# A hybrid decoder layer on one core: the linear attention's first two levels copied by another engine, its chunk states taken in one piece, and the sample products moved behind later work

## The chip, the core and the metric

The kernel runs on one core of a Trainium2 chip. The core has a matrix engine (PE, TensorE), a vector engine (DVE), an activation engine (ACT), a general engine (POOL) and a queue engine (SP) that starts DMAs. PE writes only to PSUM, which this program uses as four units of 128 partitions by 1024 floats, `unit[0]` to `unit[3]`. Each engine works through its own list of instructions in order, and the lists meet only at semaphores. The metric is the device time of one launch in microseconds; lower is better.

## What is computed

One inference step of a decoder layer for 512 prompt tokens and for 8 running sequences with 4 new tokens each ("samples"), 544 rows of width 1024. Cut to what matters here:

```python
h = x @ w_in                                        # one projection, 2320 columns
gk = log_sigmoid(g_lr @ w_gk_up + b_gk_up) / 16
# gated linear attention, 4 heads, key width 64, value width 128
S_t = diag(exp(gk_t)) S_{t-1} + k_t^T v_t ;  o_t = q_t S_t
o_gla = rms_norm(o_gla) * silu(o_gate)
o_swa = sink_attention(...)                         # window of 128 keys
x1 = layer_norm(ALPHA * x + concat(o_gla, o_swa) @ w_out)
x2 = layer_norm(ALPHA * x1 + moe(x1))               # top 4 of 32 experts
```

All products are in fp32. The recurrence also returns its last state, for the prompt and for each sample sequence.

## The kernel before

Five stages follow each other on PE: the input projections with the window attention woven in (up to 207 us of the profiled execution), the linear attention (to about 260 us), the output projection with the first layer norm and the router (to about 355 us), and then 32 experts, each with three products of 1024 by 1024 weights that stream through a ring of 16 buffers. The change touches only what lies between about 195 us and 290 us.

**Levels.** The attention matrix of a 128-token chunk is built without large exponents: for each of seven block sizes (`LEVELS`, 64 down to 1), DVE forms the exponents' arguments (`level_args(j)`), ACT takes the exponential (`level_exp(j)`), DVE multiplies keys and queries by it into `kE` and `qR` (`level_ops(j)`, which raises `ops_ready`), PE multiplies them (`level(j)`, 16 small matmuls, L1029), and DVE copies the blocks of that size under a mask into `attT` (`level_in(j)`, L2156). `E`, `kE` and `qR` exist twice, for even and odd levels. The diagonal of `attT` is written by ACT beforehand (`diagonals`, 16 copies of the identity scaled by `qkdot`), as is the samples' small `attS`. When the last level is in, DVE raises `att_ready`.

**Chunk states.** `chunk_state(i)` (L1049) multiplies the decayed keys `er` by the values `gv` for chunk i; DVE's `state_in(i)` adds them up with decay into `state`. In the kernel before they alternate with the levels, on PE and on DVE.

**Outputs.** `within_chunk(i)` (L1112) is `attT` times `gv`, `from_state(i)` (L1122) is `qe` times `state`; the samples get `sample_carried` (L1062, L1067: `qbm` times the carried state `s0`) and four products with `attS` (L1131). ACT squares each output for the norm, DVE's `norm_gate(i)` scales it. In the order 0, 1, 2, 4, 3 (`MIXED`; 4 is the samples) the rows are transposed (`mix_T`, L752), copied by ACT (`mix_in`) and multiplied by `wo` (`out_product`, L1157, L1161). `sample_state` (L1080, `kdm` times `gv`) gives the samples' new states, which DVE's `sample_state_in` adds and POOL writes out; `kdm` comes from ACT's `by_sequence`. SP starts the experts' weights only when all outputs so far are written (`out_done`).

**Units.** Which PSUM unit a result takes is written out in the tables `LATE` and `TAIL`: a result waits until the one before it in its unit has been read. At the projections' end units are released by ACT's copies of the last columns (`proj_copy(4)`, into `gv`).

ACT, PE and DVE weave pieces of the attention between the projections' steps: `piece(p)` runs after half steps, p from 0 to 39. The lines below set ACT's order at the projections' end:

```python
                if p == 37:
                    qk_in(1)
                    qk_in(2)
                    diagonals()
                if p == 38:
                    qk_in(3)
                    qk_in(4)
                    level_exp(0)
                    ...
                    by_sequence(0)
                    by_sequence(1)
```

Of the kernel before, what the change touches and what calls it, by code (L numbers as in the profile page):

```python
# [54 lines left out]
LATE = ["level0", "level1", "ds0", "level2", "ds1", "level3", "ds2", "level4", "ds3", "level5", "level_s0", "level6",  # L55
        "level_s1", "go0", "go1", "go2", "go3"]
TAIL = ["mixT0", "mixT1", "sds0", "sds1", "out0", "mixT2", "out1", "mixT4", "x1T0", "mixT3", "out2", "logit0", "x1T1", "out4", "logit1",
        "out3", "x1T2", "logit2", "x1T4", "x1T3", "logit4", "logit3"]
ORDER = ([(f"x{i}", i % 4) for i in range(NT)] + [(name, n % 3) for n, name in enumerate(LATE)] + [("go4", 3)]
         + [(name, (2, 0, 3, 1)[n % 4]) for n, name in enumerate(TAIL)]  # L60
# [59 lines left out]
def build(nc, d):  # L120
    with ExitStack() as ctx:
# [360 lines left out]
        def _(sp):  # L482
# [38 lines left out]
            sp.dma_start(res[:, 0:2], d["x_prompt"][0, 0:2 * P].rearrange("(i p) d -> p i d", p=P)).then_inc(res_in, 16)  # L521
# [220 lines left out]
        def _(pe):  # L742
# [299 lines left out]
            def chunk_state(i):  # L1042

                name = f"ds{i}"
                pe.wait_ge(*emptied(name))
                pe.wait_ge(products, NT + 2)
                for h in range(GH):
                    a, q = divmod(h, 2)
                    ins = mm(bank(name)[64 * q:64 * q + 64, a * GDV:(a + 1) * GDV], er[:, i, h * 64:(h + 1) * 64],  # L1049
                             gv[:, i, h * GDV:(h + 1) * GDV], start=True, stop=True)  # L1050
                ins.then_inc(s_full(name), 1)
# [19 lines left out]
            def sample_state(half):  # L1071

                name = f"sds{half}"
                pe.wait_ge(*emptied(name))
                pe.wait_ge(operands, 1 + half)
# [16 lines left out]
            chunk_state(1)  # L1092
            level(3)
            chunk_state(2)
            level(4)
            chunk_state(3)
            level(5)
            level(6)
            banks_free((6, 7))
            sample_carried()  # L1100
# [27 lines left out]
            within_chunk(2)  # L1128
            for h in range(GH):
# [4 lines left out]
            from_state(1)  # L1134
            from_state(2)
# [43 lines left out]
            mix_T(1)  # L1179
            sample_state(0)  # L1180
            sample_state(1)
            out_product(0)
# [226 lines left out]
        def _(act):  # L1409
# [195 lines left out]
            def diagonals():  # L1605
                act.wait_ge(used1, NIN - 2)
                act.wait_ge(qkdot_ready, 1)
                for n in range(16):
# [13 lines left out]
            def piece(p):  # L1622
# [28 lines left out]
                if p == 36:  # L1651
                    qk_in(0)
                if p == 37:
                    qk_in(1)
                    qk_in(2)
                    diagonals()
                if p == 38:
                    qk_in(3)
                    qk_in(4)
                    level_exp(0)  # L1660
                    act.wait_ge(*has(f"o{NS2 - 1}"))
                    act.wait_ge(products, NT + 2)
                    by_sequence(0)
                    by_sequence(1)
# [217 lines left out]
        def _(v):  # L1882
# [196 lines left out]
            def piece(p):  # L2079
# [27 lines left out]
                if p == 38:  # L2107
# [3 lines left out]
                    level_ops(0)  # L2111

# [60 lines left out]
            def state_in(i):  # L2173
                name = f"ds{i}"
                v.wait_ge(*filled(name))
                src = bank(name)[:, 0:2 * GDV].rearrange("p (a e) -> p a e", a=2)
# [8 lines left out]
                v.sem_inc(s_freed(name), 1)  # L2185
# [14 lines left out]
            for j in range(7):  # L2200
                if j + 2 < 7:
                    level_args(j + 2)
                if j + 1 < 7:
                    level_ops(j + 1)
                if j == 0:
                    v.wait_ge(operands, 3)
                level_in(j)
                if j == 0:
                    st(tt(qe[:], qkT[:, 0:2], eb[:], ALU.mult), queries_ready)
                    v.wait_ge(queries_ready, 2)  # L2210
                    st(tt(qbm[:], qe[:, :, SEQ:T].unsqueeze(2).to_broadcast([P, 2, NSEQ, NS]),
                          c_("colseq").rearrange("p (n t) -> p n t", n=NSEQ).unsqueeze(1)
                          .to_broadcast([P, 2, NSEQ, NS]), ALU.mult), queries_ready)
                if 1 <= j <= PT:
                    state_in(j - 1)
# [23 lines left out]
            sample_state_in(0)  # L2239
            sample_state_in(1)  # L2240
            v.wait_ge(res_in, 48)
# [58 lines left out]
            first_norm(0)  # L2300
            first_norm(1)
            first_norm(2)
# [303 lines left out]
```

## Time and profile before

| | us |
|---|---|
| median of 3 runs | 1477.77 |
| lowest, highest | 1475.67, 1478.14 |
| profiled execution, its own time | 1478.91 |
| its span, first to last instruction | 1476.8 |
| PE busy | 1401.0 (95%) |
| DVE busy, ACT busy | 470.9, 322.1 |

The profiled execution took 2.1 us more than its span; that part lies outside the instructions. Its own time is 1.1 us above the median of the runs. Times within the span are counted from the first instruction. PE is busy nearly everywhere, but the share is an average: in the stretch that the change touches it is lower, and PE runs there at half clock for most of the time.

### The profile page before, as it was taken

To read this page: it belongs to the slowest core of one execution; us is meant where nothing else is said; L and a number is where in the kernel's file an instruction comes from. 1 tells how busy PE (TensorE), PEld (TensorE's weight loads), DVE (VectorE), ACT (ScalarE), POOL (GpSimd) and SP (SyncE) were. 2 spreads that over 40 slices of the span, in tenths; PEclk is the share of its full clock that TensorE was granted. 3 is DMA by queue.
4 is the path that set the end of the run, shared out by engine and by line. 5 is a ranking of instruction groups with operands and counts; after the bars stand their busy time and mean duration, and the time that the engine had idled before them with its cause. 6 is when DMAs were issued, how large, how long until landed. Compare 5 with 4: busy or idle time off the path is not lost.

```text
span 1476.8 us, 37700 instructions
## 1 busy us (share of the span) xinstructions
PE 1401.0 (95%) x16570; PEld 956.8 (65%) x16570; DVE 470.9 (32%) x895; ACT 322.1 (22%) x662; POOL 116.0 (8%) x119
## 2 busy tenths in 40 slices
PE   6999979997999999999999999999999999999991
PEld 5777768555566666666666666666666666666660
DVE  3245547356232222223222222222322222222223
ACT  2544453321111112111111111111111111211114
POOL 1022000000010000000000000100000000010000
PEclk9999986995999999999999999999999999999996
DMA  7311032626899999999999999999999999999934
GB/s 230 101 48 44 15 122 87 246 104 252 333 373 397 400 398 396 400 390 394 399 394 395 396 399 402 398 395 391 402 399 388 397 399 398 399 401 395 389 159 143
DMA packets 78469, 463.93 MB, mean 314 GB/s; under 512 B 12401, under 2 KB 13633, under 8 KB 29009
## 3 DMA queue, kind: packets, MB, share of 16 engines
q1 hardware_dynamic: 67616, 429.54, 73.0%
q0 software_dynamic: 10192, 31.31, 8.3%
q8 instruction: 132, 2.16, 0.6%
q10 hardware_dynamic: 512, 0.79, 0.1%
q14 instruction: 17, 0.13, 0.0%
HBM read 444.70 MB, written 22.22 MB: 316 GB/s over the span
## 4 chain that ended last, share of the span: by engine, by line
PE 89%; ACT 4%; DVE 4%; DMA 2%; issue 2%; DVEq 0%; POOL 0%; ACTq 0%; SPq 0%; POOLq 0%
PE unit L1248 41%; PE unit L1251 27%; PE unit L1157 4%; PE unit L1231 2%; PE unit L757 2%; PE unit L1236 2%; PE unit L759 2%; PE unit L758 2%; PE unit L752 1%; PE unit L1175 1%; DMA xbuf<-x_prompt_dram 1%; PE unit L909 1%; PE unit L885 1%; PE unit L792 1%; PE unit L1029 0%
## 5 line engine op out<-in xcount | busy, mean ns | idle before, releaser
L1248 PE MATMUL unit<-ring_b,xeT 128*32 128x512 f32 (+1 forms) x3168 | 353.3, 488 | 1.1 <-ACT xeT L1411 1.1
L1251 PE MATMUL unit<-ring_b,xeT 128*32 128x256 f32 x1584 | 353.8, 381 | 0.0
L1251 PE MATMUL unit<-ring_a,xeT 128*32 128x256 f32 x1488 | 330.7, 379 | 0.0
L1248 PE MATMUL unit<-ring_a,xeT 128*32 128x256 f32 (+1 forms) x2976 | 330.2, 486 | 0.0
L1251 PEld LDWEIGHTS unit<-ring_b,xeT 128*32 128x32 f32 x1584 | 171.3, 110 | 56.3 <-issue 0.7
L1251 PEld LDWEIGHTS unit<-ring_a,xeT 128*32 128x32 f32 x1488 | 161.8, 110 | 52.5
L1251 PE MATMUL unit<-ring_a,heT 128*32 128x256 f32 x768 | 169.7, 379 | 0.0
L1248 PE MATMUL unit<-ring_a,heT 128*32 128x512 f32 (+1 forms) x1536 | 169.4, 486 | 0.0
L1248 PEld LDWEIGHTS unit<-ring_b,xeT 128*32 128x32 f32 x3168 | 126.4, 110 | 60.4 <-issue 4.0
L1251 PE MATMUL unit<-ring_b,heT 128*32 128x256 f32 x720 | 160.3, 379 | 0.0
L1248 PE MATMUL unit<-ring_b,heT 128*32 128x256 f32 (+1 forms) x1440 | 160.1, 486 | 0.0
L1248 PEld LDWEIGHTS unit<-ring_a,xeT 128*32 128x32 f32 x2976 | 120.1, 110 | 51.7 <-issue 2.5
L1411 ACT ACTIVATE heT<-unit 128x768 f32<-128x768 f32 x31 | 25.2, 812 | 509.6 <-PE unit L1236 509.6
L2427 DVE TENSOR_TENSOR hb<-unit,brow 128x768 f32<-128x768 f32 x32 | 30.6, 958 | 305.1 <-PE unit L1251 305.1
L2397 DVE TENSOR_TENSOR gm<-unit,brow 128x768 f32<-128x768 f32 x32 | 30.7, 958 | 233.1 <-PE unit L1251 233.1
L1251 PEld LDWEIGHTS unit<-ring_a,heT 128*32 128x32 f32 x768 | 84.3, 110 | 27.1
L694 POOL DMA_INDIRECT acc_rows<-ysb,idx x32 | 46.6, 1455 | 682.4 <-ACT ysb L1802 682.4
L1251 PEld LDWEIGHTS unit<-ring_b,heT 128*32 128x32 f32 x720 | 79.2, 110 | 25.4
L1798 ACT ACTIVATE ysb<-unit,gcol 96x768 f32<-96x768 f32 x32 | 28.7, 898 | 250.2 <-PE unit L1251 250.2
L1248 PEld LDWEIGHTS unit<-ring_a,heT 128*32 128x32 f32 x1536 | 63.0, 110 | 28.8 <-issue 0.9
L1248 PEld LDWEIGHTS unit<-ring_b,heT 128*32 128x32 f32 x1440 | 59.2, 110 | 27.9
L2327 DVE TENSOR_TENSOR row_part<-unit,ck 96x3 f32<-96x3 f32 x32 | 5.0, 155 | 209.3 <-PE unit L1225 209.3
(319 smaller groups left out, 1619.7 us busy)
## 6 DMA issues: line engine op xcount, KB each, us to landing
ring_b<-w_gate_dram SPq DMA_DIRECT2D x68, 1024.0 KB, 17.7
ring_a<-w_down_dram SPq DMA_DIRECT2D x68, 1024.0 KB, 18.2
ring_b<-w_up_dram SPq DMA_DIRECT2D x64, 1024.0 KB, 17.1
ring_a<-w_up_dram SPq DMA_DIRECT2D x64, 1024.0 KB, 18.4
ring_a<-w_gate_dram SPq DMA_DIRECT2D x60, 1024.0 KB, 17.6
ring_b<-w_down_dram SPq DMA_DIRECT2D x60, 1024.0 KB, 17.4
raw_a<-w_in_dram SPq DMA_DIRECT2D x16, 512.0 KB, 3.6
xbuf<-x_prompt_dram SPq DMA_DIRECT2D x4, 512.0 KB, 5.6
```

Source lines behind the costliest of these rows:

```text
L694: return pool.indirect_dma_start(acc_dram, bass.IndirectOffsetOnAxis(ap=at, axis=0), out, None, compute_op=ALU.add)
L757: mm(out, xh, wh, start=start, stop=False)
L758: mm(out, xh, wl, start=False, stop=False)
L759: return mm(out, xl, wh, start=False, stop=stop)
L1157: ins = mm(bank(name)[:, h * HALF:(h + 1) * HALF], mix[i % 2][:, k], wo[:, k, h * HALF:(h + 1) * HALF], start=k == 0, stop=k == KD - 1)
L1231: ins = tr(px[:, k * P:k * P + CAP], half, ident[:CAP, :CAP])
L1236: ins = tr(px[:, k * P:(k + 1) * P], gm[:, k * P:(k + 1) * P], ident)
L1248: return mm(out[j * NS:(j + 1) * NS, a:b], stat(j), w[:, a:b], start=first, stop=last)
L1251: return mm(out[CAP:P, j * 256:(j + 1) * 256], stat(j), w[:, FOLD:D], start=start, stop=stop)
L1798: nc.scalar.activation(ysb[:CAP, 0:FOLD], pd[:CAP, 0:FOLD], ACT.Identity, scale=gcol[:CAP, par:par + 1])
L2397: tt(gm[:], pg[:, 0:FOLD], brow[:, 0], ALU.add).then_inc(h_part, 1)
L2427: tt(hb[:], pu[:, 0:FOLD], brow[:, 1], ALU.add).then_inc(h_part, 1)
```

## The change

ACT's order at the projections' end is new: the diagonals are written in two halves, one after `qk_in(0)` and one ahead of `qk_in(1)`; `level_exp(0)` goes ahead of `qk_in(3)`; `by_sequence` moves behind all the exponentials. ACT copies levels 0 and 1 into `attT` itself with plain copies (`coarse_in`), two of 64x512 for level 0 and four of 32x256 for level 1; DVE does levels 2 to 6 as before. DVE computes `qe` right after the first `level_ops`, and `qbm` and the sums of the chunk states behind the levels. On PE the four chunk states form one piece between level 0 and level 1, in unit 3, which holds nothing else then. `sample_carried` moves from ahead of the outputs to behind `from_state(2)`, and `sample_state` from ahead of `out_product(0)` to behind it; DVE's `sample_state_in` moves behind the first norm. The first load of `res` signals another semaphore, so that the first two norms wait for it alone. The core of the diff:

```diff
-LATE = ["level0", "level1", "ds0", "level2", "ds1", "level3", "ds2", "level4", "ds3", "level5", "level_s0", "level6",
-        "level_s1", "go0", "go1", "go2", "go3"]
+LATE = [f"level{j}" for j in range(6)] + ["level_s0", "level6", "level_s1", "go0", "go1", "go2", "go3"]
...
             banks_free((0, 1))
             level(0)
+            banks_free((4, 5, 6, 7))
+            pe.wait_ge(proj_out, 5)
+            chunk_states()
             banks_free((2, 3))
-            level(1)
-            banks_free((4, 5))
-            pe.wait_ge(proj_out, 5)
-            chunk_state(0)
-            level(2)
...
+            for j in range(1, 7):
+                level(j)
             pe.wait_ge(att_ready, 1)
...
                 if p == 36:
                     qk_in(0)
+                    diagonals(0)
                 if p == 37:
+                    diagonals(1)
                     qk_in(1)
                     qk_in(2)
-                    diagonals()
                 if p == 38:
+                    level_exp(0)
                     qk_in(3)
                     qk_in(4)
-                    level_exp(0)
-                    act.wait_ge(*has(f"o{NS2 - 1}"))
-                    act.wait_ge(products, NT + 2)
-                    by_sequence(0)
-                    by_sequence(1)
...
+            def coarse_in(j):
+
+                half, name = LEVELS[j], f"level{j}"
+                act.wait_ge(*filled(name))
+                for q in range(2):
+                    src = bank(name)[:, q * HALF:(q + 1) * HALF].rearrange("p (b n r) -> p b n r", b=8, r=half)
+                    for n in range(64 // half):
+                        own = slice(2 * half * n, 2 * half * n + half)
+                        st(copy(attT[own, 8 * q:8 * q + 8, own.stop:own.stop + half], src[own, :, n]))
+                st.settle()
+                act.sem_inc(s_freed(name), 1)
+
+            level_exp(1)
+            level_exp(2)
+            coarse_in(0)
+            level_exp(3)
+            coarse_in(1)
             for n in range(4):
                 ins = copy(attS[:, n], ident[:NS, :NS], scale=qkdot[:NS, 16 + n:17 + n])
                 st(ins, operands if n == 3 else None)
-            for j in range(1, 7):
+            for j in range(4, 7):
                 level_exp(j)
+            act.wait_ge(*has(f"o{NS2 - 1}"))
+            act.wait_ge(products, NT + 2)
+            by_sequence(0)
+            by_sequence(1)
...
                 if j + 1 < 7:
+                    if j:
+                        v.wait_ge(*filled(f"level{j - 1}"))
                     level_ops(j + 1)
...
+                if j > 1:
+                    level_in(j)
+            for i in range(PT):
+                state_in(i)
...
             first_norm(0)
+            sample_state_in(0)
+            sample_state_in(1)
             first_norm(1)
+            v.wait_ge(res_in, 32)
             first_norm(2)
```

The first place is PE, from its first level to its first output product. In the kernel before its instructions stand so (`qR`, `kE` are a level, `gv,er` a chunk state, `s_118` the carried sample state, `gv,attT` the outputs within a chunk, `state,qe` those from the state, `gv,kdm` the new sample states):

```order
L1029 MATMUL unit<-qR,kE 128x64 x16
L1029 MATMUL unit<-qR_122,kE_121 128x64 x16
L1049 MATMUL unit<-gv,er 64x128 x4
L1029 MATMUL unit<-qR,kE 128x64 x16
L1049 MATMUL unit<-gv,er 64x128 x4
...
L1062 MATMUL unit<-s_118,zeros 32x256 x2
L1067 MATMUL unit<-s_118,qbm 32x128 x32
L1112 MATMUL unit<-gv,attT 128x128 x12
L1131 MATMUL unit<-gv,attS 32x128 x4
L1122 MATMUL unit<-state,qe 128x128 x8
```

In the changed kernel the same stretch of PE's list begins with all chunk states behind the first level, and the samples' products follow the outputs of chunks 0 to 2:

```order
L1028 MATMUL unit<-qR,kE 128x64 x16
L1049 MATMUL unit<-gv,er 64x128 x16
L1028 MATMUL unit<-qR_122,kE_121 128x64 x16
L1028 MATMUL unit<-qR,kE 128x64 x16
...
L1103 MATMUL unit<-gv,attT 128x128 x12
L1113 MATMUL unit<-state,qe 128x128 x8
L1062 MATMUL unit<-s_118,zeros 32x256 x2
L1067 MATMUL unit<-s_118,qbm 32x128 x32
L1125 MATMUL unit<-gv,attS 32x128 x4
L1103 MATMUL unit<-gv,attT 128x128 x4
```

The matmuls are the same in kind and number; the 16 of the chunk states now stand together ahead of level 1, and 34 sample matmuls stand behind `att_ready` instead of ahead of it.

The second place is ACT at the projections' end. In the kernel before, the diagonals, the keys by sequence (`kdm`) and the copies of the last projection (`gv`) stand so:

```order
L1411 ACTIVATE qTa<-unit 128x4x128 x3
L1411 ACTIVATE attT<-ck,qkdot 128x128 x16
L1411 ACTIVATE qTa<-unit 128x4x128
L1411 ACTIVATE qTa<-unit 128x4x32
L1620 ACTIVATE E<-E 128x2x512
L1411 ACTIVATE kdm<-er,ce 32x256 x8
L1411 ACTIVATE gv<-unit 128x512 x4
L1411 ACTIVATE gv<-unit 32x128 x4
L1411 ACTIVATE attS<-ck,qkdot 32x32 x4
L1620 ACTIVATE E_120<-E_120 128x2x512
```

In the changed kernel:

```order
L1403 ACTIVATE qTa<-unit 128x4x128
L1403 ACTIVATE attT<-ck,qkdot 128x128 x16
L1403 ACTIVATE qTa<-unit 128x4x128 x2
L1612 ACTIVATE E<-E 128x2x512
L1403 ACTIVATE qTa<-unit 128x4x128
L1403 ACTIVATE qTa<-unit 128x4x32
L1403 ACTIVATE gv<-unit 128x512 x4
L1403 ACTIVATE gv<-unit 32x128 x4
L1612 ACTIVATE E_120<-E_120 128x2x512
L1612 ACTIVATE E<-E 128x2x512
L1403 ACTIVATE attT<-unit 64x8x64 x2
```

The 16 diagonal copies stand two copies earlier, the first exponential two copies earlier, and nothing stands any more between the copies of the queries and keys (`qTa`) and those of the last projection.

## Rows read from the trace of the kernel before

**Rows 1.** Windows of PE: start:end, length, PE busy (count), clock share, DMA, GB/s

```profile
207.30:250.90 43.60, 33.23 (x302) 0.53 0.50 173
...
283.30:337.00 53.70, 53.59 (x240) 1.00 0.43 167
...
403.00:1476.00 1073.00, 1041.97 (x14017) 0.99 0.98 379
```

**Rows 2.** Chain that ended last, 186 to 272 us: start, length, what

```profile
201.17 4.80 ACT attT L1411 x16
...
207.93 3.28 ACT kdm L1411 x8
211.21 2.07 ACT gv L1411 x5
```

**Rows 3.** Timeline of ACT: start, length, line, operation, idle before and releaser

```profile
194.82 0.60 ACT L1411 ACTIVATE qTa<-unit 128x512 f32<-128x512 f32 x1 [0.69 <-PE unit L918]
199.67 1.32 ACT L1411 ACTIVATE qTa<-unit 128x512 f32<-128x512 f32 x2 [4.25 <-PE unit L918]
...
206.96 1.06 ACT L1620 ACTIVATE E<-E 128x1024 f32<-128x1024 f32 x1
```

**Rows 4.** Timeline of PE: last projection steps, a level, a state, outputs, products

```profile
202.67 0.96 PE L918 MATMUL unit<-ck,qk 128*128 128x128 f32 x8
...
206.55 0.65 PE L792 MATMUL unit<-raw_a,xs 128*32 128x128 f32 x16
212.26 3.68 PE L1029 MATMUL unit<-qR,kE 64*128 64x64 f32 x32 [5.07 <-ACT gv L1411]
...
221.93 1.12 PE L1049 MATMUL unit<-gv,er 128*64 128x128 f32 x8
...
248.88 4.31 PE L1067 MATMUL unit<-s,qbm 64*32 64x128 f32 x64
253.12 2.94 PE L1112 MATMUL unit<-gv,attT 128*128 128x128 f32 x24
255.99 1.06 PE L1131 MATMUL unit<-gv,attS 32*32 32x128 f32 x8
...
259.62 0.71 PE L1122 MATMUL unit<-state,qe 64*128 64x128 f32 x8
...
263.96 3.98 PE L1080 MATMUL unit<-gv,kdm 32*64 32x128 f32 x64 [0.47 <-DVEq L2231]
267.87 15.38 PE L1157 MATMUL unit<-wo,mix_a 128*128 128x512 f32 x32
...
283.96 13.90 PE L1157 MATMUL unit<-wo,mix_b 128*128 128x512 f32 x32
```

**Rows 5.** Timeline of DVE: qe, arguments, masked copies, one chunk state, the last level

```profile
219.82 1.29 DVE L2209 TENSOR_TENSOR qe<-qTa,eb 128x1088 f32<-128x1088 f32 x1
...
227.37 0.69 DVE L2059 TENSOR_TENSOR E<-cum 128x512 f32<-128x512 f32 x1
...
229.64 1.31 DVE L2156 COPY_PREDICATED attT<-ce,unit 128x512 f32<-128x512 int32 x2
231.11 0.61 DVE L2181 SCALAR_TENSOR_TENSOR state<-state,eb,unit 128x128 f32<-128x128 f32 x2 [0.16 <-DVE attT L2156]
...
247.93 2.43 DVE L2156 COPY_PREDICATED attT<-ce,unit 128x512 f32<-128x512 int32 x2 [1.02 <-PE unit L1029]
250.50 0.31 DVE L2167 COPY_PREDICATED attS<-ce,unit 32x32 f32<-32x32 int32 x2
```

**Rows 6.** Windows of PE around its clock changes, columns as in group 1

```profile
207.00:212.00 5.00, 0.19 (x8) 0.72 0.69 229
...
248.00:251.00 3.00, 3.00 (x40) 0.63 0.98 381
```

**Rows 7.** Timelines of POOL and SP: the sample states' store, the first weights

```profile
271.56 1.17 POOL L654 DMA_DIRECT2D st_s_dram<-s x1 [28.20 <-DVEq L2194]
...
277.69 1.99 SPq L543 DMA_DIRECT2D ring_b<-w_gate_dram x4
```

More of the change, by code:

```diff
@@ L520, in _ @@
             sp.wait_ge(*has("kq4"))
[L521 removed]
+            sp.dma_start(res[:, 0:2], d["x_prompt"][0, 0:2 * P].rearrange("(i p) d -> p i d", p=P)).then_inc(x_in[0], 16)
             sp.wait_ge(ops_ready, 7)
@@ L1040, in level, with chunk_states @@
                     ins.then_inc(s_full(name), 1)
-            def chunk_state(i):
-                name = f"ds{i}"
-                pe.wait_ge(*emptied(name))
+            def chunk_states():
+                pe.wait_ge(*emptied("ds"))
                 pe.wait_ge(products, NT + 2)
[L1047 to L1051, printed above, removed]
+                for i in range(PT):
+                    for h in range(GH):
+                        a, q = divmod(h, 2)
+                        at = i * 2 * GDV + a * GDV
+                        ins = mm(bank("ds")[64 * q:64 * q + 64, at:at + GDV], er[:, i, h * 64:(h + 1) * 64],
+                                 gv[:, i, h * GDV:(h + 1) * GDV], start=True, stop=True)
+                ins.then_inc(s_full("ds"), 1)
             def sample_out(a, q):
@@ L1074, in sample_state @@
                 pe.wait_ge(*emptied(name))
-                pe.wait_ge(operands, 1 + half)
+                pe.wait_ge(operands, 2 + half)
                 for n in range(4 * half, 4 * half + 4):
@@ L1128, in _ @@
             within_chunk(2)
+            from_state(1)
+            from_state(2)
+            sample_carried()
             for h in range(GH):
@@ L1179, in _ @@
             mix_T(1)
+            out_product(0)
             sample_state(0)
             sample_state(1)
-            out_product(0)
             mix_T(2)
@@ L1603, in qk_in, with diagonals @@
                 act.sem_inc(s_room(name), 1)
-            def diagonals():
-                act.wait_ge(used1, NIN - 2)
+            def diagonals(half):
+                act.wait_ge(used1, NIN - 3 + half)
                 act.wait_ge(qkdot_ready, 1)
-                for n in range(16):
+                for n in range(8 * half, 8 * half + 8):
                     st(copy(attT[:, n], ident, scale=qkdot[:, n:n + 1]))
@@ L2173, in state_in @@
             def state_in(i):
-                name = f"ds{i}"
-                v.wait_ge(*filled(name))
-                src = bank(name)[:, 0:2 * GDV].rearrange("p (a e) -> p a e", a=2)
+                v.wait_ge(*filled("ds"))
+                src = bank("ds")[:, i * 2 * GDV:(i + 1) * 2 * GDV].rearrange("p (a e) -> p a e", a=2)
                 if i == 0:
@@ L2203, in _ @@
                 if j + 1 < 7:
+                    if j:
+                        v.wait_ge(*filled(f"level{j - 1}"))
                     level_ops(j + 1)
[L2205 to L2215, printed above, removed]
+                if j == 5:
+                    v.wait_ge(operands, 1)
+                if j == 2:
+                    v.wait_ge(*emptied("level3"))
+                    v.wait_ge(*emptied("level4"))
+                if j > 1:
+                    level_in(j)
+            for i in range(PT):
+                state_in(i)
+            v.wait_ge(queries_ready, 2)
+            st(tt(qbm[:], qe[:, :, SEQ:T].unsqueeze(2).to_broadcast([P, 2, NSEQ, NS]),
+                  c_("colseq").rearrange("p (n t) -> p n t", n=NSEQ).unsqueeze(1)
+                  .to_broadcast([P, 2, NSEQ, NS]), ALU.mult), queries_ready)
             def norm_gate(i):
```

25 lines of the change are left out of this document (7 added, 18 removed).

## The prediction, made before the changed kernel ran

> **What bounds the kernel now.** I read the kernel by stretches first. From 403 us to the end PE is busy 1041.97 of 1073 us at full clock, and none of that code changes [rows 1]. From 283.3 to 337 us PE is busy 53.59 of 53.70 us: a time won before 283 us is handed on unchanged through the output products. Between 207.3 and 250.9 us it is different: PE is busy 33.2 of 43.6 us at a clock share of 0.53, so the levels are bound by something else [rows 1]. The chain of what ended last says by what. Up to about 216 us it runs through ACT: the 16 diagonals from 201.17 us for 4.80 us, `kdm` for 3.28 us, the `gv` copies from 211.21 us [rows 2]. PE had ended the projections at 207.2 us and waited 5.07 us, until 212.26 us, for a `gv` copy that frees its unit [rows 4]. From 216 us to 240 us the chain runs through DVE, which does four things for each level: arguments, operands, masked copy, chunk state. From 253 us PE's outputs take over.
>
> So there are three places to price: the start of level 0, the length of the levels up to `att_ready` (250.9 us, when the last `attS` copy of 250.50 us has ended [rows 5]), and PE's path from there to the first output product at 267.87 us [rows 4]. I make the sum against the profiled execution, 1478.91 us with a span of 1476.8, which stands 1.1 us above the median of the runs, 1477.77.
>
> **Start of level 0.** On ACT the copy of 194.82 us ends at 195.4 [rows 3]. The diagonals follow it at once, since their inputs have been there for long, and take 4.8 us as before [rows 2], to 200.3. Two `qTa` copies take 1.32 [rows 3], to 201.6, and the exponential 1.06 [rows 3], to 202.7. PE's transposes for the last two copies run from 202.67 to 203.6 [rows 4]; these copies end at about 204.3, and the `gv` copies of at most 0.6 us (five took 2.07 us, the last ones small [rows 2]) can follow the projections as they come. Level 0 needs units 0 (banks 0 and 1), free at about 205.7, and its operands: DVE starts at 204.3 and takes 1.3 for the wide `kE` (as `qe`, 1.29 for as many columns [rows 5]) and 0.7 for `qR`: 206.4. PE itself is the last, at 207.2 [rows 4]. Level 0 starts at 207.4 us, not 212.26: **4.9 us** earlier.
>
> **Levels.** DVE continues: `qe` 1.3 (207.7), arguments of level 1 behind the projections' end (209.2), arguments of level 2 (210.7), operands 1 (212.7), arguments 3 (214.2), operands 2 (215.6), arguments 4 (217.1). A pair of 0.69 us instructions with its wait is 1.4 to 1.5 us [rows 5]. PE: level 0 takes 3.68 us at half clock [rows 4]; the clock was still full until about 209 us in the row that has 0.72 for 207 to 212 us [rows 6], so I take half of it, 1.9 us, to 209.3. The 16 products of the chunk states follow: four took 1.12 us at half clock [rows 4], so 4.5 us, to 213.8. PE holds level 1 back by that: 213.8 to 217.5, level 2 to 221.2. Operands 3 overwrite the operands of level 1 and wait for it: 219.0. DVE's first masked copy, level 2, runs 221.2 to 222.7. ACT's six coarse copies are 2 times 0.6 and 4 times about 0.4 (between the 0.6 us for 512 columns and 0.27 for the small `gv` copies [rows 2]), 2.8 us in all, on an engine that is idle there; level 1's end at about 219.2, ahead of 221.2.
>
> From there DVE does 4.45 us a level (three parts) where it did 5.3 (four; a state is 0.61 plus its waits, 0.85 [rows 5]): level 3 in at 227.1, level 4 at 231.6, operands 6 at 233.1. Level 5 is filled at 233.8; its two masked copies last 2.43 us, the small ones 0.31 [rows 5]: in at 236.9. PE fills level 6 at 237.9, and it is in at **241.0**, against 250.9: 9.9 us earlier, the first 4.9 included. Bounds: had level 0 run at half clock as well, everything from level 1 on would be 1.8 us later (242.8); had PE kept full clock through the states and level 1, DVE alone would set the pace and `att_ready` come at 238.4. I take the middle because the clock had fallen at about 209 us only after PE had stood idle from 207.2, and PE is not idle there now.
>
> Here a rule can be held against the trace. PE was busy in 33.2 of 43.6 us, three quarters of the stretch, yet its clock share was 0.53 in it; it rose only at the stretch's very end, in the row of 248 to 251 us, which has 0.63 [rows 1, 6]. The Trainium skill, TensorE: Matmul & The Clock Gate (Part 1), says that the clock gate opens by how busy PE has been recently. By that sentence the denser levels would soon run at full clock, and `att_ready` would come at the 238.4 us of the bound above, 2.6 us earlier than in my sum; the two rows speak against it.
>
> **From `att_ready` to the first product.** Before, it takes from 250.9 to 260.3 us, when the last `from_state` (259.62 plus 0.71) ends: 9.4 us [rows 4]. The samples' carried products had run under DVE's last copies. Now they stand behind `att_ready`, and all is serial on PE: outputs of three chunks 2.9, two `from_state` 1.3 (0.6 to 0.7 each), the carried products 4.1 (5.0 before with the zero products, of which 2.2 us lay at half clock), `attS` 1.0, the last chunk's outputs 1.0, its `from_state` 0.6 [rows 4]: 10.9 us at full clock. DVE's four states (3.2 us) and `qbm` (0.7 us) are done at 245.0, before PE wants them. `go0`'s norm frees its unit at about 248, well ahead of the last chunk. But PE comes to this work at half clock, where before the clock had risen at 250 us under the samples' products. Bounds for the loss: 0 to all of it at half clock (below, a rival). I take 5 us at half clock, so 2.5 us, because the row of 248 to 251 us shows the rise within some 2 us of such products. End: 241.0 + 10.9 + 2.5 = 254.4, against 260.3: **5.9 us** left of the 9.9.
>
> Then the transposes. Before, three waits for DVE's norms made it 3.6 us from 260.3 to 263.96 [rows 4]. Now the norms of chunks 0 to 2 are long done; the two transposes take 2.2 us, and ACT, behind the squares of chunk 3 (to 255.7), has copied the first at 256.8. `out_product(0)` starts 2.4 us after 254.4: **1.2 us** more.
>
> **Products.** The 3.98 us of new sample states and the product swap places at the same cost. The first product took 15.3 us (to 283.2) where the later took 13.8, for PE started it at half clock [rows 4]. It now follows denser work, but the sample states may bring the same fall ahead of the second product. Between 0 and 1.5 us of gain I take 0.8.
>
> **What is hidden.** The sample states' sum moves behind the first norm, which ends at about 277 us, so their store is issued at about 280 us and not 271.56, and SP starts the experts' weights at about 286, not 277.69 [rows 7]. Seven buffers of 1 MB follow; PE wants the first at about 361, so this costs nothing. The second load of `res` waits for the sample states, too, about 6 us later than before, at 275; the store of the same megabyte was written 6.1 us after its issue [rows 7], and the third norm wants the load at about 305. Only if the cover of over 60 us were gone would this be paid in full. SP's queue holds nothing else there, and POOL's next task waits for the transpose of the samples' rows anyway.
>
> Sum: 9.9 from start and levels, less 4.0 by which the path behind `att_ready` grows (13.4 against 9.4), and 1.2 and 0.8: 7.9, rounded to **8.0 us**. 1478.9 - 8.0 = 1470.9 in a profile, 1477.8 - 8.0 = **1469.8 us** as a median.
>
> **Rivals.** (a) *Smaller gain.* All levels at half clock, level 0 too (-1.8), half clock for 8 us behind `att_ready` (-1.5), the same fall in a product (-0.8): a gain of 3.9 us, 1473.9. For it speaks the share of 0.53 in the whole stretch [rows 1]. Chance 0.24. (b) *Larger gain.* PE stays at full clock until level 1 and rises at once behind `att_ready`: 2.6 + 1.5 more, 12 us, 1465.8. Against it speaks the same row. Chance 0.13. (c) *Slower.* The clock stays low right through the outputs. Then 10.9 us become 21.8 from 242.8, to 264.6; transposes and copy 3.5, product 15.3, states 5: 288.4 against the 283.2 of before, 5 us slower, 1483. It decides from about 16 us more of half clock than my 5. For it speaks that levels that keep PE busy for three quarters of 43.6 us did not raise the clock [rows 1]; against it that it rose within some 2 us of sample products [rows 6]. Chance 0.07. (d) *No change*, within 0.2% (3 us, about what a measurement of this kernel can tell): the win is made but is taken back by something with a fixed time behind it. I find only the weights' DMA, with 60 us of cover. Chance 0.06. My forecast, a gain of 6 to 10 us, has 0.50.
>
> **How the numbers follow.** Faster by over 0.2% are the forecast, (a) but for a rest, and (b): 0.86 with the cut; same 0.07; slower 0.07. The range goes from the larger gain (1466.0) to somewhat under the smaller one (1474.8), and leaves out (c), (d) and the extremes.
>
> **What would show it.** Level 0 at about 207.4 us; DVE without masked copies until 221; PE's level 1 held by the chunk states until about 214; `att_ready` between 238.4 and 242.8; the first output product at about 257 us. A first level 0 later than 209 us, a coarse copy that ends after level 2 is filled, or a clock share near 0.5 between 245 and 257 us would make the prediction wrong.

## The result

The changed kernel took 1463.41 us in the median of 5 runs (1462.03 to 1467.1), the kernel before 1477.77 us (5 runs, 1474.71 to 1479.71). The ratio, which goes by the means, is 0.9913, with a 95% interval of 0.990 to 0.9926: 12.9 us faster, between 11 and 15. The medians are 14.4 us apart. I had forecast 1469.8 us, a gain of 8.0, and a range from 1466.0 to 1474.8. The direction was right, the gain was over half as large again as forecast, and the median lies below the range. The profiled execution took 1466.54 us.

The page of the changed kernel, its first two parts in extract (busy time, then tenths in 40 slices):

```profile
span 1464.6 us, 37705 instructions
## 1 busy us (share of the span) xinstructions
PE 1394.1 (95%) x16570; PEld 952.6 (65%) x16570; DVE 467.8 (32%) x891; ACT 325.1 (22%) x668; POOL 116.0 (8%) x119
...
PEclk8999996995999999999999999999999999999996
```

The span is 12.2 us shorter, and PE's busy time fell by 7 us although it does the same matmuls: some of them now run at full clock. DVE lost 3 us of copies and ACT gained 3, as the diff says.

The timeline of PE, from the end of the projections to the first output product (start, length, line, operation, and in brackets the idle time before it with its releaser); it answers to [rows 4]:

```profile
205.16 0.64 PE L791 MATMUL unit<-raw_a,xs 128*32 128x128 f32 x16
206.20 2.00 PE L1028 MATMUL unit<-qR,kE 64*128 64x64 f32 x32 [0.40 <-issue]
208.13 1.97 PE L1049 MATMUL unit<-gv,er 128*64 128x128 f32 x32
211.18 2.00 PE L1028 MATMUL unit<-qR,kE 64*128 64x64 f32 x32 [1.08 <-DVEq L2087]
214.14 6.63 PE L1028 MATMUL unit<-qR,kE 64*128 64x64 f32 x64 [0.95 <-DVEq L2087]
...
237.26 5.21 PE L1103 MATMUL unit<-gv,attT 128*128 128x128 f32 x24 [2.80 <-DVEq L2182]
242.40 1.16 PE L1113 MATMUL unit<-state,qe 64*128 64x128 f32 x16
...
249.61 0.71 PE L1113 MATMUL unit<-state,qe 64*128 64x128 f32 x8
...
252.81 13.97 PE L1149 MATMUL unit<-wo,mix_a 128*128 128x512 f32 x32 [0.59 <-ACT mix_a L1403]
266.71 3.71 PE L1080 MATMUL unit<-gv,kdm 32*64 32x128 f32 x64
```

Level 0 follows the projections after 0.4 us; before, it was 5.06. Level 0, the 16 chunk-state products and level 1 took 2.00, 1.97 and 2.00 us: all three at full clock. The windows of PE say when that ended (length, PE busy, clock share, DMA):

```profile
212.00:214.00 2.00, 1.18 (x22) 1.00 1.04 391
214.00:216.00 2.00, 1.86 (x23) 0.68 1.02 340
216.00:218.00 2.00, 2.00 (x22) 0.50 1.08 297
...
240.00:242.00 2.00, 2.00 (x11) 0.50 0.20 63
242.00:244.00 2.00, 2.00 (x26) 0.99 0.04 10
```

The clock fell at about 214.7 us, 8.9 us behind the projections' end, where before it had fallen 2.0 us behind it. It rose again at 242, 4.8 us into the outputs. The timeline of DVE, which answers to [rows 5], shows what came of the full clock:

```profile
215.59 0.69 DVE L2082 TENSOR_TENSOR kE<-qTa,E 128x512 f32<-128x512 f32 x1 [0.22 <-DVE E L2069]
216.20 0.68 DVE L2085 TENSOR_TENSOR qR<-qTa,E 128x512 f32<-128x512 f32 x1
217.45 1.31 DVE L2167 COPY_PREDICATED attT<-ce,unit 128x512 f32<-128x512 int32 x2 [0.56 <-PE unit L1028]
```

The first masked copy begins 11.25 us behind level 0's start; in my sum it was 13.8. The two groups of ACT's own copies, in its timeline:

```profile
210.18 1.07 ACT L1403 ACTIVATE attT<-unit 64x512 f32<-64x512 f32 x2
...
213.47 1.55 ACT L1403 ACTIVATE attT<-unit 32x256 f32<-32x256 f32 x4
```

They took 2.6 us together, against 2.8 in the sum, and were over at 215.0 us, ahead of level 2.

I compare kernels below by stages of one profile each, read from such timelines: the projections' end (end of the last product with the samples' rows), level 0's start, `att_ready` (end of the last `attS` copy), the end of the last `from_state`, the starts of the first and second output products, the experts' first product, the end of the span. All in us.

| kernel | projections end at | to level 0 | to att_ready | to last from_state | to 1st product | to 2nd product | to experts | projections' end to the end |
|---|---|---|---|---|---|---|---|---|
| before | 207.20 | 5.06 | 38.55 | 9.52 | 7.54 | 16.09 | 86.08 | 1269.60 |
| changed | 205.80 | 0.40 | 30.86 | 13.26 | 2.49 | 18.47 | 85.96 | 1258.80 |
| my sum | 207.2 | 0.2 | 33.6 | 13.4 | 2.4 | 19.4 | as before | 1261.6 |

(The last row's last entry is 1269.60 less the forecast 8.0.) Behind the projections the gain is 10.8 us; the other 1.4 us of the profiles' difference lie ahead of them, where the change moves only ACT's diagonals and first exponential.

### The profile page after: what moved, and what is told of

Same layout as the page of the kernel before. It is cut to its first block, busy times and chain, and to the rows that moved or that the text cites. A ratio compares the mean times of both kernels' runs of the same rounds, so it can differ in the third digit from the quotient of the medians.

```text
span 1464.6 us, 37705 instructions
## 1 busy us (share of the span) xinstructions
PE 1394.1 (95%) x16570; PEld 952.6 (65%) x16570; DVE 467.8 (32%) x891; ACT 325.1 (22%) x668; POOL 116.0 (8%) x119
## 4 chain that ended last, share of the span: by engine, by line
PE 90%; DVE 3%; ACT 3%; DMA 2%; issue 1%; DVEq 0%; POOL 0%; SPq 0%; ACTq 0%; POOLq 0%
PE unit L1240 42%; PE unit L1243 27%; PE unit L1149 4%; PE unit L1223 2%; PE unit L756 2%; PE unit L1228 2%; PE unit L758 2%; PE unit L757 2%; PE unit L751 1%; PE unit L1167 1%; PE unit L1028 1%; DMA xbuf<-x_prompt_dram 1%; PE unit L908 1%; PE unit L884 1%; PE unit L791 1%
```

## The experiments

Each kernel is the changed one with one edit, unless said otherwise. The stages, in the columns of the table above:

| kernel | projections end at | to level 0 | to att_ready | to last from_state | to 1st product | to 2nd product | to experts | projections' end to the end |
|---|---|---|---|---|---|---|---|---|
| before, again | 206.61 | 5.07 | 38.56 | 9.54 | 7.52 | 16.11 | 85.87 | 1269.59 |
| changed, again | 203.17 | 0.42 | 30.94 | 13.17 | 2.49 | 18.47 | 85.94 | 1258.53 |
| ACT's order undone | 203.84 | 5.08 | 30.87 | 12.75 | 2.48 | 18.47 | 85.95 | 1262.86 |
| coarse copies on DVE | 206.65 | 0.42 | 33.40 | 13.60 | 2.49 | 19.78 | 86.76 | 1264.55 |
| DVE's sums between levels | 206.48 | 0.39 | 32.64 | 12.44 | 2.49 | 18.47 | 85.90 | 1259.22 |
| states twice | 206.24 | 0.39 | 30.56 | 13.37 | 2.49 | 20.09 | 87.41 | 1261.86 |
| levels 0 to 2 and states twice | 206.23 | 0.40 | 34.49 | 13.17 | 2.49 | 18.47 | 85.97 | 1262.37 |
| matmuls into PE's waits | 201.96 | 0.40 | 33.38 | 11.01 | 2.48 | 18.71 | 87.32 | 1260.74 |
| new states first | 202.02 | 0.40 | 31.37 | 12.36 | 5.47 | 14.71 | 85.86 | 1257.58 |
| new states first, again | 206.36 | 0.40 | 30.82 | 13.30 | 5.48 | 16.36 | 85.85 | 1259.24 |
| early samples | 203.70 | 0.39 | 30.89 | 10.58 | 3.87 | 19.07 | 86.85 | 1259.10 |
| early samples, new states first | 205.98 | 0.43 | 30.96 | 10.47 | 7.10 | 14.71 | 85.19 | 1255.72 |

**The changed kernel again.** No edit.

> The changed kernel, unedited, for a second profile and more times. Two theories on why its first profile gained 12.2 us where 8.0 were forecast. Clock theory: about 2.4 us come from PE's clock staying full until level 2 (level 0 to att_ready took 31.0 us) and 1.7 us from a first output product and sample states without a half clock; both are there again, within 1.5 us. Chance theory: about 1.4 us lie ahead of 193 us, in the first loads of x, and vary from run to run, and the five first times (1462.0 to 1467.1) differ by that or by where the clock falls; then from level 0 to the experts' first product this profile stays within 1 us of the first (151.0 us), and the rest of the difference lies in the start and in the time of the clock's last rise.

Median 1466.02 us of 4 runs (1463.67 to 1467.98), ratio to before 0.9926 (0.9905 to 0.9948). From level 0 to the experts 151.01 us, against 151.04 in the first profile, the clock's fall and rise included. What differs is ahead of it: 2.6 us. So the spread of the runs lies in the start, as the chance theory had it, and the gain behind the projections is there again. Why it is there a repetition cannot say.

**The kernel before again.** No edit.

> The kernel before, unedited, for a second profile. In its first the projections ended at 207.2 us; in five profiles of changed kernels, whose code up to there is the same but for ACT's diagonals, they ended at 202.0 to 206.7 us. Chance theory: this one, too, ends them anywhere from 202 to 208 us, and from there to the end it takes 1269.6 us again, within 1 us. Rival: the change itself makes the start shorter, and it ends them at 207 us again.

1478.16 us. Behind the projections 1269.59 us, against 1269.60. The projections ended at 206.6 us, within the spread of 202.0 to 206.7 us of the changed kernels, though in its upper part, which fits both theories. Where the start's time goes shows in the windows from 150 to 180 us. Of the kernel before:

```profile
150.00:180.00 30.00, 27.61 (x159) 0.89 0.05 17
```

Of the changed kernel's second profile:

```profile
150.00:180.00 30.00, 27.55 (x165) 0.94 0.00 1
```

And of the kernel with new states first, where the code up to there is the same:

```profile
150.00:180.00 30.00, 27.56 (x173) 1.00 0.00 1
```

The projection step that runs between 159 and 176 us took 16.8, 15.4 and 13.8 us in these three. PE has waits of 0.65 and 1.45 us there while ACT and DVE take in the output gate and go on with the window attention, and the clock falls for some 7 us, some 3 us or not at all. These steps of about 1.5 us, with up to 2.6 us gathered before that step, make up the spread. Of the 2.6 us, 1.6 lie ahead of the first product of the projections, which waits for the first loads. Both profiles of before had the longest step, the two of the changed kernel one longest and one middle. With the two stages apart, the change is worth 10.8 to 11.1 us; the rest of the 12.9 lies ahead of them, where profiles of one and the same kernel spread by over 4 us. Whether ACT's earlier diagonals shift those chances stays open: 9 of 14 profiles had the longest step, and only two are of before's code.

**ACT's order undone.** This separates the late level 0 from the clock, since PE then stands idle ahead of it as before.

```diff
                 if p == 36:
                     qk_in(0)
-                    diagonals(0)
                 if p == 37:
-                    diagonals(1)
                     qk_in(1)
                     qk_in(2)
+                    diagonals(0)
+                    diagonals(1)
                 if p == 38:
-                    level_exp(0)
                     qk_in(3)
                     qk_in(4)
+                    level_exp(0)
+                    act.wait_ge(*has(f"o{NS2 - 1}"))
+                    act.wait_ge(products, NT + 2)
+                    by_sequence(0)
+                    by_sequence(1)
...
```

> ACT's order at the projections' end as before, all else as changed: diagonals behind the copies of p 37, the first exponential behind those of p 38, keys by sequence ahead of the gv copies. By my prediction level 0 starts 4.9 us later against the end of the projections (5 us behind it). Clock theory adds: PE stands idle for 5 us, so its clock falls ahead of level 0, and level 0 to att_ready takes about 3 to 4 us more than the 31.0 us of the changed kernel, since level 0 (3.7), the states (4.5) and level 1 run at half clock. In all about 8 us later at att_ready. Rival: the levels are paced by DVE alone, and it takes 31 us again, 5 us later in all.

1468.63 us. Level 0 started 5.08 us behind the projections, 4.7 later, as both theories had it. But `att_ready` came after the same 30.87 us: the clock theory's extra 3 to 4 us did not come. The timeline of PE in this kernel:

```profile
208.92 3.68 PE L1028 MATMUL unit<-qR,kE 64*128 64x64 f32 x32 [5.08 <-ACT gv L1403]
212.53 3.68 PE L1049 MATMUL unit<-gv,er 128*64 128x128 f32 x32
216.14 5.91 PE L1028 MATMUL unit<-qR,kE 64*128 64x64 f32 x96
```

And DVE's first masked copy:

```profile
220.17 1.33 DVE L2167 COPY_PREDICATED attT<-ce,unit 128x512 f32<-128x512 int32 x2 [0.33 <-PE unit L1028]
```

Level 0 and the states ran at half clock (3.68 us each, where they took 2.00 and 1.97). DVE was no further ahead: the operands of levels 1 and 2 were there 5.0 and 8.0 us behind level 0's start, against 4.8 and 7.7. But PE had no wait from 208.92 us on, and levels 1 and 2 ran at full clock, so that level 2 was filled 11.2 us behind level 0's start, as in the changed kernel, where PE had waited 1.08 and 0.95 us. The experiment shows that half clock in level 0 and the states costs nothing while levels 1 and 2 run at full clock; it says nothing on half clock in those. It also gave a price: 16 chunk-state products in a row take 3.68 us at half clock, not four times the 1.12 of [rows 4].

**Chunk states issued twice.** This gives the states the time that my sum had for them.

```diff
-                for i in range(PT):
+                for i in 2 * list(range(PT)):
```

> The 16 products of the chunk states are issued twice (same result), so that they take 4.0 us at full clock instead of 2.0. This sets PE's time between level 0 and level 1 nearly to what my prediction had (4.5 us). Theory that this term was the mis-sized one: level 1 starts 0.9 us later than its operands, level 2 is filled later by as much or more, and att_ready comes 1 to 2.5 us later than the 30.9 us behind level 0. Rival, DVE paces the levels and PE's time does not matter: 30.9 us, within 0.3.

1470.03 us. Level 1 started 0.8 us behind its operands, but `att_ready` came after 30.56 us, no later than in the changed kernel. The timeline of PE has both levels at full clock:

```profile
212.21 2.00 PE L1028 MATMUL unit<-qR,kE 64*128 64x64 f32 x32
214.57 2.00 PE L1028 MATMUL unit<-qR,kE 64*128 64x64 f32 x32 [0.36 <-DVEq L2087]
```

The rival's number came: the states' length alone is not the failed term. But the clock stayed full until 218.5 us here, through all of level 2, so this holds for short levels behind long states and not for the half-clock levels of my sum. (Its longer whole comes from a fall of the clock, from 269.7 to 276.5 us, ahead of and under the second product.)

**Levels 0 to 2 issued twice as well.** On top of the last edit:

```diff
-                for a in range(2):
+                for a in range(2) if j > 2 else (0, 1, 0, 1):
```

> Levels 0 to 2 and the chunk states are all issued twice (same results), so that they take at full clock what my prediction gave them at half clock: level 0 4.0 us, states 3.7, levels 1 and 2 4.0 each. Theory that the failed term is PE's time for levels 1 and 2: level 2 is filled about 2.5 us later, DVE's first masked copy starts 13.5 to 15 us behind level 0's start instead of 11.2, and att_ready comes at 33.5 to 35 us behind it instead of 30.9. Rival: DVE paces all of it, 30.9 us again.

1470.54 us. `att_ready` came 34.49 us behind level 0, 3.6 later. The timeline of DVE:

```profile
217.83 0.69 DVE L2082 TENSOR_TENSOR kE<-qTa,E 128x512 f32<-128x512 f32 x1 [2.02 <-PE unit L1028]
218.44 0.69 DVE L2085 TENSOR_TENSOR qR<-qTa,E 128x512 f32<-128x512 f32 x1
221.51 1.31 DVE L2167 COPY_PREDICATED attT<-ce,unit 128x512 f32<-128x512 int32 x2 [2.38 <-PE unit L1028]
```

DVE now waits twice for PE, 2.02 us for level 1's operands to be read and 2.38 for level 2 to be filled, and its first masked copy starts 14.9 us behind level 0. These are the two waits of my sum. Level 0 was doubled as well and took 3.8 us, where my sum had 1.9; so the first copy comes 1.1 us later than the sum's 13.8, and `att_ready` 0.9 later than its 33.6. Against the run with only the states doubled the levels' length costs 3.9 us. PE's time up to the end of level 2 is the term that was mis-sized, and the length of the levels decides in it.

**Coarse copies on DVE.** Both `coarse_in` calls are gone, and DVE copies all levels under its masks.

```diff
-            coarse_in(0)
...
-            coarse_in(1)
...
-                if j > 1:
-                    level_in(j)
+                level_in(j)
```

> DVE copies levels 0 and 1 under its masks again, ACT none. If DVE paces the levels throughout, att_ready comes 2 x 1.45 = 2.9 us later than in the changed kernel. Rival: DVE's wait for level 2 (0.56 us) and the waits at the last two levels (0.96 us each) take a part up, and it is 1 to 2 us.

1473.2 us. `att_ready` 2.5 us later, between the two. The timeline of DVE has level 0's copy between the operands of level 1 and the arguments of level 3:

```profile
211.97 1.34 DVE L2165 COPY_PREDICATED attT<-ce,unit 128x512 f32<-128x512 int32 x2
213.46 0.69 DVE L2066 TENSOR_TENSOR E<-cum 128x512 f32<-128x512 f32 x1
```

Each pair of copies takes 1.5 us of DVE's time with its wait; the missing 0.4 us of the 3.0 lay in DVE's wait for level 2, 0.56 us in the changed kernel and gone here. The further 3 us of this run come from the clock, which fell from 273.6 to 280.4 us and again at 335 us.

**DVE's sums between the levels.** `state_in(j - 1)` behind each of the copies 1 to 4 again.

```diff
-            for i in range(PT):
-                state_in(i)
...
+                if 1 <= j <= PT:
+                    state_in(j - 1)
```

> DVE sums the chunk states between the levels' copies again (one behind each of levels 1 to 4), PE's order as changed. If DVE paces the levels, att_ready comes up to 4 x 0.85 = 3.4 us later behind level 0's start than 30.9 us, less the 0.6 to 1.3 us that DVE waits for level 2; that is what moving the sums was worth. Rival: the sums fall into DVE's waits for PE at levels 2, 5 and 6 and cost less than 1.5 us.

1467.68 us. `att_ready` came 1.8 us later, between the two theories. The four sums added 2.9 us to DVE's work, and its waits for PE shrank by 1.2: from 0.56 to 0.25 us at level 2, from 0.96 to 0.22 at level 5, from 0.96 to 0.85 at level 6. The outputs were 0.8 us faster, because the clock rose 3.3 us behind `att_ready` and not 4.9. So 0.9 us are left at the experts' first product, and 0.4 at the end.

**Matmuls into PE's waits.** If half clock costs time in the outputs, keeping PE busy should give it back. The added products write where the next result starts anew.

```diff
+            def warm(name, times):
+                pe.wait_ge(*emptied(name))
+                for _ in range(times):
+                    mm(bank(name)[:, 0:HALF], ident, gv[:, 0], start=True, stop=True)
...
             for j in range(1, 7):
+                if j > 1:
+                    warm(f"level{j}", (0, 1, 2, 2, 2, 2)[j - 1])
                 level(j)
+            warm("go0", 3)
             pe.wait_ge(att_ready, 1)
```

> Matmuls whose result nobody reads (identity times values, 512 columns) fill PE's waits: one ahead of level 2, two ahead of each of levels 3 to 6, three ahead of the outputs, each into the unit that the next result takes. Clock theory: PE stays at full clock, the levels' end is 2 us earlier (the two waits of 0.96 us at levels 5 and 6 go), the outputs take 10.9 instead of 13.1 us: 4 us faster than the changed kernel, about 1460. Rival: the clock falls as before; then each level is held up by the added matmuls (1.7 us each at half clock on top of 3.7), and it is 3 to 6 us slower.

Median 1464.19 us of 4 (1463.39 to 1465.14), ratio 0.9909 (0.989 to 0.9928). From level 0 to the experts it took 152.9 us, 1.9 longer than in the changed kernel: the added products do not pay. Each theory holds for one part. The timeline of PE:

```profile
209.28 1.97 PE L1095 MATMUL unit<-gv,ck 128*128 128x512 f32 x2
211.18 3.68 PE L1028 MATMUL unit<-qR,kE 64*128 64x64 f32 x32
214.79 3.78 PE L1095 MATMUL unit<-gv,ck 128*128 128x512 f32 x4
...
235.95 2.94 PE L1113 MATMUL unit<-gv,attT 128*128 128x128 f32 x24
```

The clock fell at 209.4 us all the same, 7.4 us behind the projections' end, and until 219.7 us the added products cost twice their length and held levels 2 and 3 up: `att_ready` 2.5 us later. From then on PE stayed at full clock up to 267.4 us, beyond the first product, and the outputs took 2.94 and not 5.21 us; the path behind `att_ready` was 11.0 us, the 10.9 of my sum without its half-clock term. That term, 2.5 us in the sum, is thereby shown: 13.2 against 11.0, 2.2 us.

**New states first.** The swap undone:

```diff
+            sample_state(0)
+            sample_state(1)
             out_product(0)
-            sample_state(0)
-            sample_state(1)
...
```

The sum of the sample states on DVE and the order of the units go back with it.

> The samples' new states go ahead of the first output product again, on PE and on DVE, in units 3 and 0. By my prediction the swap itself is worth about nothing: from the last from_state to the second output product (21.0 us in the changed kernel) it takes 21 us plus up to 1 us for the norms that free those units. Rival: the swap is what kept the clock up, the clock falls as before under the first product and it is 1.6 to 2.5 us more. The experts' first weights would be issued some 6 us earlier, with no effect.

> New states first, again, timed. Theory: 149.8 us from level 0 to the experts' first product against 151.0 us of the changed kernel (within 0.7 us), median about 1 us below that of the changed kernel, which its times (spread 1462 to 1468 us) hardly tell apart. The clock's fall in the projections (150 to 180 us) and the first loads move each run by up to 5 us: the profile's time from 159 to 175 us or less tells which.

The first run took 1461.4 us; the second time, in 6 runs, the median was 1467.13 us (1462.37 to 1467.7), ratio 0.9925 (0.9911 to 0.9939). From the last `from_state` to the second product it took 20.2 and 21.8 us, against 21.0 in the changed kernel. Without the fall of the clock that the second profile has, from 256.3 to 259.7 us inside the first product, the old order is 0.8 us faster; the sample states fill the 0.59 us in which PE waits for ACT's copy. The swap is worth nothing, or less. The times cannot tell the kernels apart.

**Early samples.** Of 13 us behind `att_ready` over 4 are the carried products, while PE waits 2.80 us just ahead of it. For this ACT copies the chunk states out of unit 3, and `qbm` is formed where DVE waits for level 5.

```diff
             coarse_in(0)
+            act.wait_ge(*filled("ds"))
+            st(copy(dsb[:].rearrange("p i a e -> p (i a e)"), bank("ds")[:]), cache_T_ready)
+            act.wait_ge(cache_T_ready, 3)
+            act.sem_inc(s_freed("ds"), 1)
...
             for j in range(1, 7):
                 level(j)
+            sample_carried()
             pe.wait_ge(att_ready, 1)
...
```

> The samples' carried products go ahead of att_ready again, into the 2.8 us in which PE waits for the last masked copies. For that ACT copies the chunk states from unit 3 to SBUF (one more copy of 1.0 us), DVE sums them from there, and qbm is formed ahead of level_in(5), where DVE waits. Theory: of the path of 13.2 us behind att_ready 4.1 us go, PE comes about 1.5 us late from them, and the clock rises earlier: 2.5 to 4 us faster than the changed kernel. Rival: at half clock the products take 5 us and more, hold the outputs up by 3 us, and it is less than 1 us.

Median 1465.19 us of 4 (1464.58 to 1466.9), ratio 0.9919 (0.9891 to 0.9947). The path behind `att_ready` fell to 10.6 us, by 2.6 to 2.7. But from level 0 to the experts it took 151.3 us, against 151.0: the 2.5 to 4 us that I had expected did not come, though not for the rival's reason. Its timeline shows where they went:

```profile
244.85 0.71 PE L1115 MATMUL unit<-state,qe 64*128 64x128 f32 x8
247.16 0.63 PE L752 MATMUL unit<-ck,og 128*128 128x128 f32 x4 [1.60 <-DVEq L2250]
```

PE now outruns ACT's squares and DVE's norms, and waits 1.60 us for a unit ahead of the transposes; a fall of the clock at 267.3 us took the rest.

**Early samples and new states first.** Both edits together.

> Early samples and samples' new states ahead of the first product together. Early samples alone took 2.6 us off the path behind att_ready and gave 1.4 of them back in a wait for DVE's norms ahead of the transposes; new states first alone was 0.8 us faster from the last from_state to the second product. Theory: together, from level 0 to the experts' first product 149 us, about 2 us below the changed kernel and 0.5 to 1 us below new states first alone. Rival: the waits for the norms add up and it is no faster than new states first alone (149.8 us).

Median 1463.56 us of 4 (1462.9 to 1463.93), ratio to before 0.9907 (0.9893 to 0.9922). Its profile takes 1255.72 us from the projections' end to the end, 2.8 to 3.1 us less than the changed kernel's two, and 148.4 us from level 0 to the experts. In that measure it beats the other kernels here, as expected. It is a single profile, and one in which the clock did not fall between the outputs and the experts, as it did in some others. The median lies in the changed kernel's spread; the profiled run had the longest step of the projections.

## Why the prediction was wrong, and where it was right

The start of level 0: right. 4.66 us against 4.9, and the experiment that undoes ACT's order gives 4.7 back. The order of steps on ACT was as written.

The levels: this step failed. I let PE hold the levels back, "213.8 to 217.5, level 2 to 221.2", on the ground that the clock would fall at about 209 us as it had before. It fell at 214.7 us. Levels 1 and 2 did not end 10.1 and 13.8 us behind level 0's start but at about 7.0 and 11.2, DVE's first masked copy came 2.5 us earlier, and `att_ready` after 30.9 and not 33.6 us. Three of PE's times went into it: the states (4.5 us taken, 1.97 measured), level 1 (3.7 taken, 2.00 measured) and level 2 (3.7 taken, 3.3 measured, part of it at half clock). The states' length alone makes no difference, as issuing them twice shows. With levels 0 to 2 doubled as well the forecast's two waits are back, and 3.6 us. No run has long levels behind short states, so what each would cost alone stays open. From the first masked copy on the sum was right: 19.6 us to `att_ready`, against 19.8. My own bound had held the case (238.4 us, "had PE kept full clock through the states and level 1"): 31.0 us behind level 0, and 30.9 were measured. I gave it a chance of 0.13, together with a clock that rises at once behind `att_ready`, which did not come (it rose 4.9 us behind it), because the clock share of the whole stretch was 0.53; but that stretch began with 5 us of an idle PE, which the change removes. The row for 207 to 212 us [rows 6] said that the fall had followed the idle time, and I named this and then took a middle all the same.

As for the rule of the Trainium skill (TensorE: Matmul & The Clock Gate, Part 1), that the clock gate opens by how busy PE has been: for the first levels the trace agrees, since PE, busy behind the projections, kept full clock for 8.9 us. For the later ones it does not: at 222 to 234 us PE was busy in over 90% of the time at a share of 0.50.

The path behind `att_ready`: right in sum and parts. 13.26 us against 13.4; the half-clock term of 2.5 us measured 2.2. The 5 us at half clock in it were a choice between bounds, so that this came out so close is in part luck. Rival (b) was added up too low: a rise at once gives back the whole 2.5 us, not 1.5, and makes its gain 13.1 us.

To the second output product: 21.0 us against 21.6 by the sum's gains, 21.8 in its own steps (2.4 to the first product, 14.5 for it, 4.0 for the new states, 0.9 for the next transposes). The first product ran at full clock all through, 13.9 us, and the new states took 3.7 us. Against before's 23.6 us the gain is 2.7, where I had summed 2.0: here the term for the clock, 0.8 of a possible 1.5 us, was too small.

Hidden work: right. The states' store was issued at 275.7 us and the experts' weights at 281.8; from the second product to the experts' first it took 85.96 us, against 86.08.

The part that no step had: 1.4 us of the profiles' difference lies ahead of the change, in the first loads (the first product of the projections starts at 22.5 us before and at 21.1 in the changed kernel), and the medians differ by more, since the runs of either kernel spread over 5 us. I took the median of three runs as a fixed base, and gave a range of 9 us for the sum with no share for the start. The sum of stages: 1.4 start, 4.7 to level 0, 7.7 levels, -3.7 behind `att_ready`, 2.7 to the second product, 0.1 to the experts, and -0.6 in the experts, whose clock rose 1 us later than before: 12.2 us. My sum had 4.9, 5.0, -4.0 and 2.0 for the four stages in the middle. These stages alone would have left the median in the range: 1477.77 less the 10.8 us won behind the projections is 1467.0. Of the other 3.6 us between the medians the profiles show 1.4, in a stage that the change does not touch; the rest no profile shows.

## What to carry to other kernels

When a change removes an idle time of PE, do not price what follows at the clock that the idle time had caused: price it at both levels, and ask which wait each one brings. Where two engines take turns, doubling one's work in place is a cheap test of whether its length matters: here states doubled cost nothing, and levels 0 to 2 doubled with them 3.6 us. Look, too, at what the doubling does to the clock. And compare profiles from the last common point before the change on, since the start spreads by more than many changes are worth.

## What the runs showed of the hardware

In the three profiles in which PE stood idle for 5.1 us behind the projections (both of before, and ACT's order undone) the clock fell 2.0 to 2.3 us behind their end. In the other eleven level 0 followed within 0.43 us, and the clock stayed full for 7.4 to 19.2 us.

In both kernels the clock stayed at 0.50 through levels 4 to 6, though PE was busy in over 80% of that time (in the changed kernel from 226.5 to 234.4 us without a gap), and rose 2 to 5 us into the products behind them; with ACT's order undone it rose 7.5 us behind the start of level 0, with no gap in PE's work. It fell, too, while PE worked: at 267 us in the kernel before, at the end of the new sample states and after four waits of 0.4 to 0.6 us, and at 256 us in one run of the changed order but not in another of the same code. Such falls lasted 3.4 to 6.8 us, and each cost 1.4 to 3.1 us. So the same code took 13.8, 15.4 or 16.8 us in one projection step.
